# Half of an MLP input by seven block products of eight, in a fused decoder layer on one core

## The reference

```
h = rms_norm(x, pre_norm_mix);  y = hybrid_mixer(h, ...)       # attention and gated delta rule
x = x + rms_norm(y, post_norm_mix)
h = rms_norm(x, pre_norm_mlp)
y = square(relu(h @ w_mlp_in)) @ w_mlp_out                     # 1024 -> 4096 -> 1024
x = x + rms_norm(y, post_norm_mlp)
```

## Time and profile before

| | us |
|---|---|
| median of three runs | 750.17 |
| profiled execution, own time | 749.34 |
| its span, first to last instruction | 747.6 |
| TensorE busy | 740.2 |
| VectorE, ScalarE, GpSimd busy | 435.5, 389.5, 324.9 |

### The profile page before, as it was taken

How to read it: one execution, slowest core, us unless ns; L and a number is a source line. 1 busy time by engine, 2 the same in 40 slices (tenths; PEclk the granted TensorE clock), 3 DMA queues, 4 the chain that set the end, 5 groups by cost and what they waited for, 6 DMA issues and landing times.

```text
span 747.6 us, 11913 instructions
## 1 busy us (share of the span) xinstructions
PE 740.2 (99%) x4168; PEld 607.8 (81%) x4168; DVE 435.5 (58%) x651; ACT 389.5 (52%) x632; POOL 324.9 (43%) x296
## 2 busy tenths in 40 slices
PE   9999999999999999999999999999999999999996
PEld 7788778888877878788888988888888888888885
DVE  5897899980454545444983512221221777778795
ACT  6657842268554365635655733333332655555671
POOL 2348894435454754574536466546545000000002
PEclk9999999999999999999999999999999999999999
DMA  9436224456476597276650279979978575554652
GB/s 330 113 87 211 57 71 114 127 128 150 132 171 156 169 198 197 64 160 202 210 185 28 85 233 274 238 227 294 237 227 216 159 228 194 198 184 154 220 174 114
DMA packets 86302, 129.22 MB, mean 173 GB/s; under 512 B 6096, under 2 KB 45168, under 8 KB 86256
## 3 DMA queue, kind: packets, MB, share of 16 engines
q1 hardware_dynamic: 76384, 109.47, 45.8%
q0 software_dynamic: 9536, 18.88, 14.8%
q10 hardware_dynamic: 336, 0.28, 0.1%
HBM read 126.49 MB, written 39.86 MB: 223 GB/s over the span
## 4 chain that ended last, share of the span: by engine, by line
PE 93%; POOL 3%; ACT 2%; DVE 1%; DMA 0%; issue 0%; SPq 0%; POOLq 0%; ACTq 0%; DVEq 0%
PE bank L767 28%; PE bank L768 27%; PE bank L769 27%; POOL rsq L2167 2%; PE bank L1014 1%; PE bank L1037 1%; PE bank L1024 1%; POOL w_lo L2173 1%; PE bank L978 1%; PE bank L788 1%; PE bank L942 1%; PE bank L794 1%; PE bank L989 1%; PE bank L797 0%; PE bank L1076 0%; DMA raw<-in_w_in 0%
## 5 line engine op out<-in xcount | busy, mean ns | idle before, releaser
L2173 POOL TENSOR_TENSOR w_lo<-raw,w_hi 128x512 fp32r<-128x512 f32 x169 | 219.4, 1308 | 232.7 <-ACT w_hi L1229 230.7
L1229 ACT ACTIVATE w_hi<-raw 128x512 fp32r<-128x512 f32 (+2 forms) x214 | 145.1, 684 | 154.6 <-PE bank L769 126.5
L767 PE MATMUL bank<-h_hi,w_hi 128*128 128x512 f32 (+1 forms) x528 | 208.6, 395 | 0.2
L768 PE MATMUL bank<-h_lo,w_hi 128*128 128x512 f32 (+1 forms) x528 | 204.2, 387 | 0.0
L769 PE MATMUL bank<-h_hi,w_lo 128*128 128x512 f32 (+1 forms) x528 | 204.1, 387 | 0.0
L767 PEld LDWEIGHTS bank<-h_hi,w_hi 128*128 128x128 f32 x528 | 99.2, 188 | 26.1 <-issue 5.1
L769 PEld LDWEIGHTS bank<-h_hi,w_lo 128*128 128x128 f32 x528 | 99.2, 188 | 20.5
L768 PEld LDWEIGHTS bank<-h_lo,w_hi 128*128 128x128 f32 x528 | 99.3, 188 | 18.6
L1638 DVE SCALAR_TENSOR_TENSOR relu_sb<-bank,rs_row 128x512 f32<-128x512 f32 x32 | 20.6, 686 | 126.5 <-PE bank L769 114.8
L2311 POOL TENSOR_SCALAR ssh<-ssy 128x1 f32<-128x1 f32 x4 | 1.0, 238 | 151.6 <-ACT junk L1609 151.6
L767 PE MATMUL bank<-w_hi,a_hi 128*128 128x512 f32 x120 | 46.8, 390 | 0.0
(11 more groups left out here) (327 smaller groups left out, 1268.0 us busy)
## 6 DMA issues: line engine op xcount, KB each, us to landing
raw<-in_w_in SPq DMA_DIRECT2D x87, 256.0 KB, 2.9
raw<-in_w_mlp_in SPq DMA_DIRECT2D x62, 256.0 KB, 4.9
t_sum<-in_w_mlp_out POOLq DMA_DIRECT2D x12, 1024.0 KB, 10.7
raw<-in_w_mlp_out SPq DMA_DIRECT2D x26, 256.0 KB, 3.1
raw<-t_sum SPq DMA_DIRECT2D x26, 256.0 KB, 3.2
v_sum<-in_w_mlp_out SPq DMA_DIRECT2D x4, 1024.0 KB, 6.5
t_sum<-in_w_mlp_out SPq DMA_DIRECT2D x4, 1024.0 KB, 7.2
v_sum<-in_w_mlp_out POOLq DMA_DIRECT2D x4, 1024.0 KB, 11.4
```

Source lines behind the costliest of these rows:

```text
L767: pe.matmul(o, s_hi, m_hi, start=start, stop=False, skip_group_check=True)
L768: pe.matmul(o, s_hi, m_lo, start=False, stop=False, skip_group_check=True)
L1229: return a.activation(o, i_, ACT.Copy, scale=scale)
L2173: g.tensor_tensor(w_lo[:, slot, :], raw[:, slot, :], w_hi[:, slot, :].bitcast(F32), ALU.subtract).then_inc(lo_ready, 1)
```

## The change

The first eight groups of the MLP input (2048 features) stay as they are. The other 2048 features are treated as two halves of 1024 (`F_HALF`), h as 2 x 2 blocks (features by tokens, 512 x 256 each), and the product as seven block products (q1 to q7) of eight. It goes in four steps (`STEPS_IN`) of 256 features of each half; a step has 14 units (`PER_STEP`) of twelve matmuls that move 256 tokens. q1, q2 and q4 use blocks of w_mlp_in; q5, q7, q6 and q3 use four sums of its blocks (`u_sum`, 2 MB each), which SP copies and GpSimd adds in the mixer (`IN_SUM_AT`, `IN_ADD_AT`). On the other side q6, q7, q4 and q5 use four combinations of h's blocks, which VectorE makes from sums of `h_hi` and `h_lo` (`full_block`, `t_blocks_made`) and which are split again (`block_high` on ScalarE, `t_low` on VectorE) during the last plain groups.

Results are put together from PSUM: ScalarE copies q1 to `p1`; VectorE makes e1 = p1 - q6, f1 = p1 + q5, c11 with its relu in one operation, c22, c12 and c21 into `relu_sb`, and one relu for the other three blocks (`relu_in`) at the start of the next step. Squares follow in `square_in`. TensorE's products wait for these by the counter `made_in`.

Raw tiles come from a ring of eight in the steps (`raw_of`); a load waits for the low part of eight units before. Of the 14 low parts of a step GpSimd makes four (`LOW_POOL`) and VectorE ten.

The sums of w_mlp_out pair other rows for the second half of features (`w2_block`, `w2_late`), and are spread anew: three chunks in the mixer (six before), five in the plain groups, the rest in the steps and in the MLP output (`copy_sum` on SP, `add_sum` on GpSimd). The combinations of h lie where x stood, so x is copied to HBM in groups 2 and 3 and loaded again by GpSimd's queue in the MLP output, and with it post_norm_mlp (`late_in`). The loops over groups of the MLP input and over SP's parts are shorter or written out. Some semaphores are shared under new names.

The diff, cut to its core:

```diff
--- before.py
+++ after.py
...
-U_M1 = U_OUT + 64
+G_PLAIN = 8
+F_HALF = (FF - G_PLAIN * 256) // 2
+U_S = U_OUT + 4 * G_PLAIN
+STEPS_IN = F_HALF // 256
+PER_STEP = 14
+RING = 8
+CHUNKS = F_HALF // 512
+U_M1 = U_S + STEPS_IN * PER_STEP
...
-OUT_SUM_AT = {48: 0, 52: 1, 60: 2, 87: 3}
+OUT_SUM_AT = {60: 0, 63: 1, 68: 2, 72: 3}
 OUT_ADD_AT = {u + 2: q for u, q in OUT_SUM_AT.items()}
-SUM_AT = {61: (0, 0), 65: (1, 0), 73: (2, 0), 74: (0, 1), 78: (1, 1), 86: (2, 1)}
+SUM_AT = {84: (0, 0), 89: (1, 0), 94: (0, 1)}
 ADD_AT = {u + 2: chunk for u, chunk in SUM_AT.items()}
-SUM_IN = {2: (0, 2), 3: (0, 3), 4: (3, 0), 5: (3, 1), 7: (2, 2), 8: (2, 3), 9: (1, 2), 10: (1, 3), 12: (3, 2), 13: (3, 3)}
+IN_SUM_AT = {10: (0, 0), 14: (0, 1), 34: (1, 0), 42: (1, 1), 50: (2, 0), 56: (2, 1), 75: (3, 0), 79: (3, 1)}
...
-SUM_IN = {2: (0, 2), 3: (0, 3), 4: (3, 0), 5: (3, 1), 7: (2, 2), 8: (2, 3), 9: (1, 2), 10: (1, 3), 12: (3, 2), 13: (3, 3)}
+IN_SUM_AT = {10: (0, 0), 14: (0, 1), 34: (1, 0), 42: (1, 1), 50: (2, 0), 56: (2, 1), 75: (3, 0), 79: (3, 1)}
+IN_ADD_AT = {u + 2: chunk for u, chunk in IN_SUM_AT.items()}
+SUM_IN = {2: (2, 0), 3: (1, 1), 4: (2, 1), 5: (0, 2), 7: (1, 2)}
...
+IN_PRODUCTS = ("q1", "q6", "q5", "q2", "q7", "q3", "q4")
+T_ORDER = (3, 0, 1, 2)
+IN_BANK = {"q1": 0, "q2": 0, "q6": 2, "q7": 2, "q4": 2, "q5": 4, "q3": 4}
+LOW_POOL = (1, 3, 7, 11)
+LOW_DVE = tuple(v for v in range(PER_STEP) if v not in LOW_POOL)
...
+def made(name, s, e):
+    return 14 * s + 2 * ("e1", "f", "c11", "c22", "c12", "c21", "relu").index(name) + e + 1
...
+    def u_copy(q, chunk):
+        return u_block(q, chunk), (w1_block(0, 1, chunk), w1_block(0, 0, chunk), u_block(0, chunk), u_block(2, chunk))[q]
+    def u_add(q, chunk):
+        return u_block(q, chunk), w1_block(*((1, 1), (0, 1), (0, 0), (1, 0))[q], chunk)
+    def in_source(s, v):
+        name, half = IN_PRODUCTS[v // 2], v % 2
+        if name in ("q1", "q2", "q4"):
+            k_half, f_half = {"q1": (0, 0), "q2": (1, 0), "q4": (1, 1)}[name]
+            r0, c0 = k_half * 512 + half * 256, G_PLAIN * 256 + f_half * F_HALF + 256 * s
+            block = w_mlp_in[0][r0:r0 + 256, c0:c0 + 256]
+        else:
+            block = u_sum[{"q5": 0, "q7": 1, "q6": 2, "q3": 3}[name]][half * 256:half * 256 + 256, 256 * s:256 * s + 256]
+        return block.rearrange("(k p) c -> p k c", p=P)
...
+        for s in range(STEPS_IN):
+            for v in range(PER_STEP):
+                u = U_S + PER_STEP * s + v
+                if v >= RING - RAW or s:
+                    sp_.wait_ge(*low_of(u - RING))
+                dst = raw_of(u).rearrange("p (k c) -> p k c", k=2)
+                sp_.dma_start(dst, in_source(s, v)).then_inc(raw_signal(u)[0], 16)
+                if (s, v) == (0, 8):
+                    copy_sum(0, 3)
+                if (s, v) == (2, 0):
+                    copy_sum(2, 2)
...
+        def in_product(s, name):
+            if name == "q1":
+                pe.wait_ge(made_in, made("c11", s - 1, 1)) if s else pe.wait_ge(relu_done, 2 * G_PLAIN - 2)
+            elif name == "q6":
+                pe.wait_ge(made_in, made("c21", s - 1, 1)) if s else pe.wait_ge(relu_done, 2 * G_PLAIN)
+            elif name == "q5" and s:
+                pe.wait_ge(made_in, made("c12", s - 1, 1))
+            elif name == "q2":
+                pe.wait_ge(p1_copied, 2 + 2 * s + 2)
+            elif name == "q7":
+                pe.wait_ge(made_in, made("e1", s, 1))
+            elif name == "q3":
+                pe.wait_ge(made_in, made("f", s, 1))
+            elif name == "q4":
+                pe.wait_ge(made_in, made("c22", s, 1))
+            if s == 0 and name == "q6":
+                pe.wait_ge(dlo_ready, 2 * OUT_G + 4)
+            for half in range(2):
+                u = U_S + PER_STEP * s + 2 * IN_PRODUCTS.index(name) + half
+                pe.wait_ge(*low_of(u))
+                for kk in range(2):
+                    for e in range(2):
+                        c = slice(kk * 256 + e * P, kk * 256 + e * P + P)
+                        x_ = three(bank[IN_BANK[name] + e][:, 0:256], w_hi[:, u % SPL, c], w_lo[:, u % SPL, c],
+                                   *in_operand(name, 2 * half + kk), name in ("q1", "q6", "q5") and half + kk == 0,
+                                   name in ("q2", "q4", "q3") and half + kk == 2)
+                x_.then_inc(unit_done, 1)
...
+        def square_in(s, e):
+            a.wait_ge(made_in, made("relu", s, e))
+            for m in range(2):
+                a.activation(act_pair(G_PLAIN + 2 * s + e, slice(4, 6) if m else slice(0, 3, 2)),
+                             relu_sb[:, 2 * e + m, :].rearrange("p (s c) -> p s c", s=2), ACT.Square).then_inc(act_ready, 1)
+        def mlp_in_step(s):
+            for v in range(PER_STEP):
+                u = U_S + PER_STEP * s + v
+                if u + LEAD < U_M1:
+                    split_in(u + LEAD)
+                else:
+                    a.wait_ge(unit_done, u)
+                    w_split(u + LEAD - U_M1, 1, 16)
+                if v == 2:
+                    if s:
+                        a.wait_ge(made_in, made("c21", s - 1, 1))
+                    for e in range(2):
+                        copy(p1[:, e, :], bank[e][:, 0:256]).then_inc(p1_copied, 1)
+                if s and v in (3, 4):
+                    square_in(s - 1, v - 3)
+                if s == STEPS_IN - 1 and v == 8:
+                    a_split(0, 0, slice(0, 4))
...
         a_split(1, 1, slice(0, 4))
-        square_group(NI - 1, 1)
         w_split(6, 2, 16)
+        for e in range(2):
+            square_in(STEPS_IN - 1, e)
...
+        def t_blocks_made():
+            n["dve_chain"] = n.get("dve_chain", 0) + 4
+            v.wait_ge(dve_chain, n["dve_chain"])
+            b11, b12, b22, b21 = [t[:] for t in h_full]
+            mark(v.tensor_tensor(t_full[3][:], b11, b12, ALU.subtract), diffs_made)
+            mark(v.tensor_tensor(t_full[0][:], b22, t_full[3][:], ALU.add), diffs_made)
+            mark(v.tensor_tensor(t_full[1][:], b12, b22, ALU.subtract), diffs_made)
+            mark(v.tensor_tensor(t_full[2][:], b21, t_full[0][:], ALU.subtract), diffs_made)
...
+        def c21(s, e):
+            v.tensor_tensor(relu_sb[:, 2 * e + 1, 0:256], bank[2 + e][:, 0:256], p1[:, e, :], ALU.subtract).then_inc(made_in, 1)
+        def relu_in(s, e):
+            v.wait_ge(made_in, made("c21", s, 1))
+            r_ = relu_sb[:, 2 * e:2 * e + 2, :].rearrange("p m c -> p (m c)")[:, 256:]
+            stt(r_, r_, 0.0, rs_ext[:], ALU.max, ALU.mult).then_inc(made_in, 1)
+        def step_in(s):
+            for v_ in range(PER_STEP):
+                u = U_S + PER_STEP * s + v_
+                if v_ == 0 and s:
+                    v.wait_ge(unit_done, u)
+                    for e in range(2):
+                        c21(s - 1, e)
+                if v_ == 1 and s:
+                    for e in range(2):
+                        relu_in(s - 1, e)
+                if v_ == 4:
+                    v.wait_ge(unit_done, u)
+                    v.wait_ge(p1_copied, 2 + 2 * s + 2)
+                    for e in range(2):
+                        v.tensor_tensor(e1[:, e, :], p1[:, e, :], bank[2 + e][:, 0:256], ALU.subtract).then_inc(made_in, 1)
+                if v_ == 6:
+                    v.wait_ge(unit_done, u)
+                    for e in range(2):
+                        v.tensor_tensor(f1[:, e, :], p1[:, e, :], bank[4 + e][:, 0:256], ALU.add).then_inc(made_in, 1)
+                if v_ == 8:
+                    v.wait_ge(unit_done, u)
+                    for e in range(2):
+                        v.wait_ge(act_ready, 2 * (G_PLAIN - 2 + 2 * s + e) + 2)
+                        stt(relu_sb[:, 2 * e, 0:256], bank[e][:, 0:256], 0.0, rs_row[:, 0:256], ALU.max, ALU.mult).then_inc(made_in, 1)
+                if v_ == 10:
+                    v.wait_ge(unit_done, u)
+                    v.wait_ge(made_in, made("f", s, 1))
+                    for e in range(2):
+                        v.tensor_tensor(relu_sb[:, 2 * e + 1, 256:512], bank[2 + e][:, 0:256], f1[:, e, :], ALU.subtract).then_inc(made_in, 1)
+                if v_ == 12:
+                    v.wait_ge(unit_done, u)
+                    for e in range(2):
+                        v.tensor_tensor(relu_sb[:, 2 * e, 256:512], bank[4 + e][:, 0:256], e1[:, e, :], ALU.add).then_inc(made_in, 1)
+                in_low(u + LEAD)
+                if v_ in (7, 9):
+                    combine_in(G_PLAIN - 2 + 2 * s + v_ // 2 - 3)
+                if s == STEPS_IN - 1 and v_ == 10:
+                    a_low(0, 0, slice(0, 4), 1)
+                if s == STEPS_IN - 1 and v_ in (12, 13):
+                    w_low(v_ - 12, 1, v_ - 11)
...
+        w_low(2, 1, 3)
+        v.wait_ge(unit_done, U_M1)
+        for e in range(2):
+            c21(STEPS_IN - 1, e)
         w_low(3, 1, 4)
         w_low(4, 2, 6)
         a_low(1, 1, slice(0, 4), 2)
+        for e in range(2):
```

(21 more changed lines are left out.)

301 lines of the change are left out of this document (216 added, 85 removed).

## The result

The changed kernel takes 765.03 us (median of five executions, 757.99 to 767.09) against 750.15 before: 1.0191 times the time, 95% interval 1.0145 to 1.0237. It is slower; the forecast was 744.6. The profiled execution is the fastest of the five (757.99, span 756.2), so its waits are probably shorter than usual.

What follows compares the result with a forecast made beforehand. TensorE was taken to bound the kernel (busy 740.2 of 747.6 us). 749.34 - 6.7 + 0.1 + 1.0 = 743.8, and 744.6 with the median 0.83 us above the profiled run; range 743.2 to 749.0.

Steps and rivals of the forecast that it cites:

- step 5: DMA transfers: loads still land in time; 0, bounds 0 and +4 us in the steps, 0 and +3 in the output.
- Step 1: TensorE's MLP input: 87.3 us of plain groups go, 80.6 us of 256-column matmuls come; -6.7 us.
- Step 2: Queues of ScalarE, VectorE and GpSimd within the steps: nothing late, cost 0; upper bound +9 us.
- the cover of 1.16 us: In a step's queue layout, VectorE finishes c22 1.16 us before TensorE wants it at q4; called the thinnest cover.
- the exclusion of rows 7: VectorE and GpSimd operations waiting for each other's end: a VectorE 128x256 subtraction took 1.54 instead of 0.42 us.
- Step 3: Entering the steps from the last plain group: +0.1 us, bounds 0 and 0.6; h block work hidden.
- Step 4: Leaving the steps for the MLP output: third activation set's low part late, +1.0 us once, bounds 0 and 2.3.
- Step 6: Mixer, with five more adds by GpSimd and five more copies by SP: 0, bounds 0 and +2 us.
- the danger: Rival: VectorE and GpSimd delay each other at every meeting in the steps; 9 us, 753.5 us; chance 8%.
- loads late: Rival: loads land late behind the 1 MB copies in the steps; +3 us, 747.6 us; chance 12%.

Runs made afterwards that it cites:

- e14: Kernel before plus only six 1 MB copies and six adds into unread memory, at the changed kernel's places in its output: 761.17 us, 1.0141.
- e9: Changed kernel without the sums of mixer, steps and MLP output (other blocks read instead), reload of x after 24 output parts: 749.18 us, 0.9994.
- e12: e9 with e4's edit, and x not stored in the plain groups but reloaded from its input: 748.45 us, 0.9976.
- e3: Changed kernel with the mixer's first three sum copies moved from units 10, 14, 34 to 30, 33, 37: 767.26 us, 1.0229.
- e7: Changed kernel without the mixer's eight copies and adds of w_mlp_in sums, output's sums kept: 762.96 us, 1.0189.
- e10: Changed kernel with the reload of x and the norm weights moved behind the add of sum (3, 2): 763.76 us, 1.0197.
- e11: Changed kernel with each of the output's six sum copies and adds split into two half-size transfers, one unit apart: 783.11 us, 1.0453.
- e1: Changed kernel without the MLP output's six sum copies and six adds (other rows read instead): 757.56 us, 1.0100.
- e2: Changed kernel with sums moved: w_mlp_in's to units 31 to 55, eleven w_mlp_out chunks into the mixer, none in steps or output: 780.70 us, 1.0398.
- e4: Changed kernel with the last two relus and their four squares moved behind the second set of output parts: 767.68 us, 1.0263.
- e5: Changed kernel without the mixer's eight and the MLP output's six copies and adds of sums: 752.79 us, 1.0036.
- e6: Changed kernel with the activation's split and low part before the weight splits, in the output's first pass: 767.18 us, 1.0245.
- e8: The changed kernel again, unchanged, timed beside its variants: 763.35 us, 1.0184 against the kernel before.
- e13: Changed kernel with the output's six sum copies issued by GpSimd, each followed by its add, reload of x behind all: 769.42 us, 1.0254.

## Why the prediction was wrong

The step that failed is step 5, the transfers: put at 0 in the output, with bounds 0 and +3, where they cost 6.6 us in the fastest execution and 11 by e14. The steps one by one:

- **Step 1** (TensorE, -6.7): held. 256-column starts are 0.120 us apart in the long stream too, and e9 and e12 have 80.6 and 80.7 us for the steps. The Trainium skill's page "TensorE: Matmul & The Clock Gate", section "Back-to-back issue gap", from which I had an estimate of a 15.6 us loss, is again not what the chip showed (0.120 us at 256 columns, 0.227 at 512).
- **Step 2** (the step's queues, 0): held without a copy in the step, failed with one. c22 was 1.22 us late once, in step 0. ScalarE had stood 1.62 and 2.63 us for loads of sums (513.98, 517.24), GpSimd 3.05 us in front of its add; the cover of 1.16 us was gone. VectorE's 128x256 subtraction at 519.59, beside GpSimd's low part, took 1.52 instead of 0.42 us, the exclusion of rows 7. The Trainium skill's page "SBUF — State Buffer", section "Who interferes with whom", has it so, and the trace agrees. In e9, without the copy, step 0 has no wait.
- **Step 3** (entering, +0.1): 0 in the first profile, e3, e7, e9, e10 and e11, 0.96 to 1.0 in e1, e2, e4, e5, e6, e8, e12 and e13, for VectorE's first low part of the steps (504.95 in e5), which stands behind the four low parts of the h blocks. I had reckoned these at 1.2 to 1.3 us, hidden; two of them take 1.22, and the two beside GpSimd's low parts 2.3 us, 6.8 together.
- **Step 4** (leaving, +1.0, bounds to 2.3): 2.1 to 2.7 us, around or over its upper bound. I had reckoned without ScalarE's 2.36 us of waiting for raw_c, which can be issued only at the output's start; the squares that filled that time before now stand behind it. With e4's order it was 1.14.
- **Step 5** (transfers, 0 in the steps and 0 to +3 in the output): this is the step that failed. Of the 9.7 us by which the output grew in the fastest execution, 2.3 are the exit's wait (step 4) and 6.6 the four waits behind it (with 0.16 us for each); e14 has some 11 from the transfers alone. In the steps they cost c22's 1.22. I had the share right (full at times), and called it covered by "eight slots ahead (10.9 us) and their splits another six ahead". That counts cover which a stream has only once. A buffer is refilled only behind its own low part, so a late landing makes the next load of that buffer late as well. With issue, split and low part (about 3 us) a round of 10.9 us bears landings of about 8 us one after the other, and the second pass, whose round is six parts and 8.2 us, about 5. In the kernel before the longest was 5.0; beside the sums the median alone is 5.3 to 6.0, and the tail 8 to 11.5. Before, 10 of the sums stood in the plain groups, where a landing of 9.7 us was seen and cost nothing; I took that as proof for a stretch with other buffers.
- **Step 6** (mixer, 0 to +2): +3.1 us, in e8 +6.0, of which some 1.2 are the wait near 390 that the change did not bring. GpSimd's adds did not wait, as I had argued. But at 55 us TensorE waits because VectorE was held for 3.85 us beside an add (e3), and at 67 us because a load took 8.27 us (57.26). I had priced GpSimd's time for the issues (1.26 us each), neither what they do to VectorE nor the bytes. SyncE's side held: it waited 17.2 us once for a sum to land, in front of no wait of TensorE.

What I named as the danger (VectorE and GpSimd holding each other up at every meeting in the steps) did not come there; they do hold each other up in the mixer, beside an add. The rival "loads late" had 12%, +3 us, and stood in the steps, not in the output. The book for e8's profile, 18.8 us over before: its 17 waits of 18.8 us, with 0.16 us each, make 21.5; the lower clock behind 726 us adds 1.4, and TensorE's work takes off 6.7. That is 16.2; 2.6 us, in delays too small to list, are not placed.

Without the sums of w_mlp_in and with eight of the sixteen chunks of sums of w_mlp_out the change is worth 0.9976 at best (e12), and that flatters it: e9 and e12 move 123.0 and 120.9 MB, less than the kernel before with 129.2. Even so they gain 0.8 and 1.6 us of the 5.6 that were forecast; waits at the entry and the exit and the one at 388 take much of the rest. What e9 and e12 leave out then costs 14 to 17 us, two to two and a half times TensorE's 6.7. A version that computes the layer and beats the kernel before was not found, and no run points to one.

Open: whether smaller transfers without waits in SyncE's queue would be cheaper (e11 and e13 each changed more than that), and whether the loads are late for want of the DMA engines' time or for something else that the transfers share. The share was 0.93 to 1.06 where they were late, and 0.56 before.

## What to carry to other kernels

An algorithm that trades matmuls for sums in memory pays in bytes: put the transfers alone into the old kernel first (e14); that one run foretells the loss in the output. Price a transfer by what lands late beside it, with the round of a buffer (issue + landing + split + low part) against the time in which the buffer comes round, for each pass by itself: here 10.9 and 8.2 us. A stretch at a DMA share of 0.56 is no room for 60 us of transfers when a buffer's round there bears landings of some 5 us and some land in 5.0 already. Before crediting an engine's name in a wait, follow the chain: behind VectorE's name stood a load at 658 us, and behind GpSimd's name VectorE at 55.

## What had not been expected of the hardware

- A wait of TensorE of 1.8 to 4.7 us was often, not always, followed by 1.7 to 5.6 us, mostly 3, with starts 0.43 us apart instead of 0.23: granted clock at the lower of the two levels (1.2 GHz). Behind 2.70 us in e1 and 1.79 in e4 (664 us) it came, behind 2.18 and 2.40 in the first profile and 2.83 in e10 it did not. Each such stretch costs 0.8 to 2.6 us, mostly about 1.4.
- In the sixteen profiles, 26 VectorE operations ran over 2 us longer than the shortest of their kind (3.7 to 7.1 us instead of 0.2 to 1.2), none of them in the kernel before or in e14. Every one began 0.2 to 1.2 us behind the start of GpSimd's issue of an add. Most adds are not followed by one.
- A timeline row that stands for two issues (x2) is not the price of two issues. SyncE's row at 515.36 spans 3.63 us and the one at 659.41 in e8 3.88 us, but the issues in them took 0.92 and 0.37, and 0.44 and 0.32 us; between them SyncE waited for a buffer. The 2.50 and 3.88 us in e10's expectation are such rows.
- The same kernel varies more once transfers decide: before, 748.8 to 750.5 us in all runs; changed, 758.0 to 768.1; e14, 756.3 to 763.1.
